# Decode trunk on Trainium2: wider moving operands in the sampled compression, chunk numbers made two stages earlier, gate products spread differently

## What is computed

```python
def compress_blocks(rows, w1, b1, w2):          # CMP_STRIDE 16, CMP_RATIO 2
    chunks = rows.reshape(b, n_chunks, CMP_STRIDE, g, d)
    part = jnp.einsum('bcjgd,ujde->ubcge', chunks, w1)
    hid = b1 + part[0, :, :n_cmp]
    for u in range(1, CMP_RATIO):
        hid = hid + part[u, :, u:u + n_cmp]
    return jnp.einsum('bcge,ef->bcgf', jax.nn.silu(hid), w2)

def full_rows(cache, new):
    past = cache[page_table].reshape(b, past_len, N_KV, HEAD_DIM)
...
    kc = compress_blocks(full_rows(ck_c, k_c), w1[0], b1[0], w2[0])
    vc = compress_blocks(full_rows(cv_c, v_c), w1[1], b1[1], w2[1])
```

## Time and profile before

| what | value |
|---|---|
| median of 3 runs | 2046.36 us (2042.62 to 2046.47) |
| the profiled execution's own time | 2048.14 us |
| its span | 2046.1 us |
| PE busy | 1841.1 us (90%) |
| DVE, ACT, POOL busy | 680.1, 560.5, 368.8 us |
| `compress_sample` in the trace | about 1139 to 1342.6 us |
| `attend_sample` in the trace | about 1342.6 to 1533 us |

### The profile page before, as it was taken

The page is one execution under the profiler, slowest core; times in us unless marked ns, Lnnn a source line. Parts: engine busy times, 40 slices in busy tenths (PEclk is TensorE's granted clock), DMA queues, the critical chain, the costliest instruction groups (busy, mean ns, idle before and its releaser), DMA issues. The chain is left out here.

```text
span 2046.1 us, 42386 instructions
## 1 busy us (share of the span) xinstructions
PE 1841.1 (90%) x18840; PEld 1228.6 (60%) x18840; DVE 680.1 (33%) x1448; ACT 560.5 (27%) x1148; POOL 368.8 (18%) x438
## 2 busy tenths in 40 slices
PE   7999689999999979689888489888999999899997
PEld 5666465666666645556666478875666666444443
DVE  3101354344443235066666445244120010111122
ACT  4111433334331200166665011122220000122223
POOL 0211331122220000044545211013200010000000
PEclk9999699999999989799999799888999999999999
DMA  4110100000000061350000775436732110400110
GB/s 138 52 31 11 28 3 12 22 13 13 12 13 23 14 149 21 134 125 2 2 2 1 226 231 178 177 101 147 174 85 103 42 41 21 166 21 21 41 41 21
DMA packets 116074, 135.96 MB, mean 66 GB/s; under 512 B 48220, under 2 KB 97061, under 8 KB 111326
## 3 DMA queue, kind: packets, MB, share of 16 engines
q1 hardware_dynamic: 106576, 83.95, 14.9%
q0 software_dynamic: 9216, 49.29, 7.7%
q10 hardware_dynamic: 102, 0.03, 0.0%
HBM read 120.64 MB, written 16.62 MB: 67 GB/s over the span
## 5 line engine op out<-in xcount | busy, mean ns | idle before, releaser
L709 PE MATMUL ps<-xnT,rw_side_w 128*128 128x344 f32 x576 | 202.3, 474 | 0.0
L448 PE MATMUL ps<-xnT,w_z 128*128 128x344 f32 x624 | 183.7, 456 | 2.3 <-DVE xnT L541 1.3
L448 PEld LDWEIGHTS ps<-xnT,w_z 128*128 128x128 f32 x624 | 118.9, 192 | 63.9 <-issue 3.1
L1822 POOL TENSOR_SCALAR probs<-probs,row_sums,gates 128x63 f32<-128x63 f32 (+6 forms) x148 | 95.0, 657 | 291.6 <-DVE row_sums L1782 291.6
L709 PEld LDWEIGHTS ps<-xnT,rw_side_w 128*128 128x128 f32 x576 | 99.5, 190 | 44.6 <-issue 11.1
L2094 PE MATMUL ps<-xnT,zT 128*128 128x344 f32 x384 | 123.9, 473 | 0.0
L2578 PE MATMUL ps<-xnT,ring_k 128*128 128x344 f32 x384 | 116.7, 458 | 2.2 <-PEq L81 2.2
L2582 PE MATMUL ps<-zT,ring_k 128*128 128x344 f32 x384 | 115.0, 452 | 0.0
L2762 PE MATMUL ps<-w_pg,h_T 128*128 128x512 f32 x256 | 111.3, 593 | 1.0 <-ACT h_T L2791 1.0
L2706 PE MATMUL ps<-w_out,mT 128*128 128x512 f32 x256 | 111.6, 593 | 0.5 <-DVE h_sample L2846 0.5
L1166 POOL TENSOR_TENSOR rw_Lb<-rw_Lm,level_mask 128x512 f32<-128x512 f32 x40 | 50.6, 1273 | 271.2 <-DVE rw_Lm L1325 261.2
(11 more groups left out here) (512 smaller groups left out, 2932.5 us busy)
## 6 DMA issues: line engine op xcount, KB each, us to landing
w_z<-in_w_in_dram SPq DMA_DIRECT2D x13, 512.0 KB, 3.8
xnT_kept<-xnT SPq DMA_DIRECT2D x1, 4128.0 KB, 12.7
xnT<-xnT_kept SPq DMA_DIRECT2D x1, 4128.0 KB
x_tok<-in_x_prompt_dram SPq DMA_DIRECT2D x8, 512.0 KB, 7.9
rw_side_w<-in_w_in_dram SPq DMA_DIRECT2D x16, 256.0 KB, 3.3
zT<-in_w_in_dram SPq DMA_DIRECT2D x8, 512.0 KB, 8.7
ring_k<-in_w_in_dram SPq DMA_DIRECT2D x8, 512.0 KB, 4.1
w_out<-in_w_out_dram SPq DMA_DIRECT2D x1, 4096.0 KB
```

The lines of the kernel that those rows point to most:

```text
L448: last = nc.tensor.matmul(k.ps[:, u % 6, 0:CG], w[:, n % w_ring, c, :], k.xnT[:, c, g * CG:(g + 1) * CG], start=(c == 0), stop=(c == KC - 1))
L709: ins = nc.tensor.matmul(k.ps[:, SIDE_BANKS[g % 2], 0:CG], w.side[:, t % 2, c, :], k.xnT[:, c, g % 3 * CG:(g % 3 + 1) * CG], start=(c == 0 ...
L1822: nc.gpsimd.tensor_scalar(every, every, ls[:, at:at + 1], k.gates[:, i, gate:gate + 1], ALU.mult, ALU.mult).then_inc(scaled, 1)
```

## The change

1. `convolve` takes both head groups in one moving operand of 256 columns. A pass is now half of the 16 token positions for one half of the channels: 8 x 4 matmuls, 4 passes, so 128 matmuls per unit. `project` still stands after the second pass and `score` after the third.
2. The chunk numbers are made in `turn_rows`. The tables and the page table are loaded by SP in `project_tokens`; PE's turn and spread stand after the second and fifth group of transposes in `turn_rows`. `compress_sample` starts with the gathers.
3. SP holds back the 16 transfers `cmp_w1v` until DVE has turned the first 4 gathers (`tr` 4).
4. In `attend_sample` 8 products more stand in `FILL_SELECT`, 8 new ones (`FILL_INDEX`) after the spread of the chosen rows, and 2 + 2 fewer in each of the 4 parts. `FILL_END` stays 16.

```diff
@@ project_tokens, SP
             sp.dma_start(k.dist_near[:], x.tab["dist"][:, W_SEL:]).then_inc(in_dist, 16)
+            sp.dma_start(k.pages_i[:], x.page_table).then_inc(in_page, 16)
+            for n in PAGE_TABLES:
+                sp.dma_start(k.tab[n][:], x.tab[n]).then_inc(in_page, 16)
             one.spread(sp)
@@ turn_rows, PE
                 last.then_inc(turned, 1)
+                if u == 1:
+                    pe.wait_ge(paged, 1)
+                    nc.tensor.transpose(k.ps[0:NPAGE, 5, 0:NB], k.pages[:], k.ident[0:NB, 0:NB]).then_inc(pt_ps, 1)
+                if u == 4:
+                    pe.wait_ge(paged, 2)
+                    for hf in range(2):
+                        last = nc.tensor.matmul(k.ps[:, 6, hf * NB:(hf + 1) * NB], k.tab["page_of"][:, hf, :], pages_t[:],
+                                                start=True, stop=True)
+                    last.then_inc(ix_ps, 1)
@@ turn_rows, DVE
+            nc.vector.tensor_copy(k.pages[:], k.pages_i[:]).then_inc(paged, 1)
             for u in range(1, 8, 2):
                 dve.wait_ge(turned, u + 1)
                 nc.vector.tensor_copy(k.kT[:, u // 2, 512:1024], k.ps[:, u % 4, :]).then_inc(out_v, 1)
+                if u == 1:
+                    dve.wait_ge(pt_ps, 1)
+                    nc.vector.tensor_copy(pages_t[:], k.ps[0:NPAGE, 5, 0:NB]).then_inc(paged, 1)
+            dve.wait_ge(ix_ps, 1)
+            for hf in range(2):
+                nc.vector.tensor_scalar(k.chunk_idx[:, hf, :], k.ps[:, 6, hf * NB:(hf + 1) * NB], 8.0, k.tab["mod8"][:, 0:1],
+                                        ALU.mult, ALU.add).then_inc(out_v, 1)
@@ compress_sample, SP
-            sp.dma_start(pt_i[:], x.page_table).then_inc(in_pt, 16)
             for n in CHUNK_TABLES:
                 sp.dma_start(k.tab[n][:], x.tab[n]).then_inc(in_tab, 16)
+            sp.wait_ge(tr, 4)
             assert load_block_weights(sp, x, w1[1], 1, in_w) == BLOCK_DMAS
@@ compress_sample, POOL
-            pool.wait_ge(idx_ok, 2)
@@ compress_sample, PE
-            def convolve(v, g, dh):
-                kv, s = units[v][0], v % 2
-                for j in range(16):
+            def convolve(v, part):
+                kv, s, dh = units[v][0], v % 2, part // 2
+                for j in range(8 * (part % 2), 8 * (part % 2) + 8):
                     for i in range(4):
                         h = slice(32 * i, 32 * i + 32)
-                        last = nc.tensor.matmul(k.ps[:, 4 * s + i, g * P:(g + 1) * P],
-                                                w1[kv][h, j, dh, :, :].rearrange("p u e -> p (u e)"),
-                                                ct[s][h, 4 * j + 2 * g + dh, :, :].rearrange("p m b -> p (m b)"),
+                        last = nc.tensor.matmul(k.ps[:, 4 * s + i, 0:256], w1[kv][h, j, dh, :, :].rearrange("p u e -> p (u e)"),
+                                                ct[s][h, 4 * j + dh:4 * j + dh + 3:2, :, :].rearrange("p g m b -> p g (m b)"),
                                                 start=(dh == 0 and j == 0), stop=(dh == 1 and j == 15))
...
-                convolve(v, 0, 0)
-                convolve(v, 0, 1)
+                convolve(v, 0)
+                convolve(v, 1)
                 if v:
                     project(v - 1)
-                convolve(v, 1, 0)
+                convolve(v, 2)
                 if v and units[v - 1][0] == 0:
                     score(v - 1)
-                convolve(v, 1, 1).then_inc(conv, 1)
+                convolve(v, 3).then_inc(conv, 1)
@@ attend_sample
-FILL_SOFT, FILL_SELECT, FILL_SPREAD = 8, 16, 8
-FILL_KEYS, FILL_SCORE, FILL_TURN = (4, 4, 4, 2), 8, 4
+FILL_SOFT, FILL_SELECT, FILL_INDEX, FILL_SPREAD = 8, 24, 8, 8
+FILL_KEYS, FILL_SCORE, FILL_TURN = (4, 4, 3, 1), 8, 3
...
+            mg.products(pe, FILL_INDEX)
             pe.wait_ge(w_lowd, 1)
...
-            mg.copies(act, FILL_SELECT)
+            mg.copies(act, FILL_SELECT + FILL_INDEX)
```

More of the change, by code:

```diff
@@ L252, in _ @@
             sp.wait_ge(in_dist, 32)
+            sp.wait_ge(in_page, 16 * (1 + len(PAGE_TABLES)))
         @block.tensor
@@ L337 @@
 RW_TABLES = ("ident2", "upper1", "lower", "level_mask", "gmask", "chunk_mask", "q_scale")
+PAGE_TABLES = ("page_of", "mod8")
 EARLY_TABLES = RW_TABLES + ("seen", "q_unscale")
@@ L1427, in turn_rows @@
         turned, out_a, out_v, gated = ctx.sem("rows_turned"), ctx.sem("rows_by_act"), ctx.sem("rows_by_dve"), ctx.sem("gates")
+        paged, pt_ps, ix_ps = ctx.sem("pages_float"), ctx.sem("pages_turned"), ctx.sem("pages_spread")
+        pages_t = ctx.enter_context(nc.sbuf_tensor("pages_t", [NPAGE, NB], F32))
         block = ctx.enter_context(nc.Block())
@@ L1870, in compress_sample @@
         kcT = sb("s_kcT", [P, 2, 256])
-        in_pt, in_tab, in_later, in_w, in_xn = (ctx.sem(n) for n in ("in_pages", "in_tab", "in_later_tabs", "in_cmp_w1v", "in_xnT"))
+        in_tab, in_later, in_w, in_xn = (ctx.sem(n) for n in ("in_tab", "in_later_tabs", "in_cmp_w1v", "in_xnT"))
         in_c = [ctx.sem(f"in_chunks{n}") for n in range(ring)]
-        prep, zeroed, pt_ps, ix_ps, idx_ok, qz, tr, conv, fd, hd, sd, w2p, w2o, scd, sco = (ctx.sem(n) for n in (
-            "sc_prep", "sc_zeroed", "pages_turned", "pages_spread", "idx_ready", "q_spread", "c_turned",
+        zeroed, qz, tr, conv, fd, hd, sd, w2p, w2o, scd, sco = (ctx.sem(n) for n in (
+            "sc_zeroed", "q_spread", "c_turned",
             "c_conv", "c_first", "c_hidden", "c_silu", "c_w2", "c_w2_out", "c_scored", "c_scores_out"))
@@ L2017, in _ @@
         def _(dve):
-            dve.wait_ge(in_pt, 16)
-            nc.vector.tensor_copy(pt_f[:], pt_i[:]).then_inc(prep, 1)
-            dve.wait_ge(pt_ps, 1)
-            nc.vector.tensor_copy(pt_t[:], k.ps[0:NPAGE, 4, 0:NB]).then_inc(prep, 1)
-            dve.wait_ge(in_tab, 16 * len(CHUNK_TABLES))
-            for hf in range(2):
-                dve.wait_ge(ix_ps, 2)
-                nc.vector.tensor_scalar(idx[:, hf, :], k.ps[:, 5, hf * NB:(hf + 1) * NB], 8.0, k.tab["mod8"][:, 0:1], ALU.mult,
-                                        ALU.add).then_inc(idx_ok, 1)
             dve.wait_ge(zeroed, 3)
@@ L2050, in scores @@
                 dve.wait_ge(scd, v + 1)
+                if v == 0:
+                    dve.wait_ge(in_tab, 16 * len(CHUNK_TABLES))
                 for bb in range(2):
@@ L2107, in copies @@
         self.out += count
-FILL_SOFT, FILL_SELECT, FILL_SPREAD = 8, 16, 8
-FILL_KEYS, FILL_SCORE, FILL_TURN = (4, 4, 4, 2), 8, 4
-FILL_END = 3 * KC * KC - 3 * FILL_SOFT - FILL_SELECT - 2 * FILL_SPREAD - 4 * (sum(FILL_KEYS) + FILL_SCORE + 2 * FILL_TURN)
+FILL_SOFT, FILL_SELECT, FILL_INDEX, FILL_SPREAD = 8, 24, 8, 8
+FILL_KEYS, FILL_SCORE, FILL_TURN = (4, 4, 3, 1), 8, 3
+FILL_END = 3 * KC * KC - 3 * FILL_SOFT - FILL_SELECT - FILL_INDEX - 2 * FILL_SPREAD - 4 * (sum(FILL_KEYS) + FILL_SCORE + 2 * FILL_TURN)
 def load_merge_weights(sp, k, x, f):
@@ L2947, in hybrid_trunk @@
         k.q_s = sb("q_s", [P, NPAIR, NB])
+        k.pages_i, k.chunk_idx = (early.enter_context(nc.sbuf_tensor(n, shape, I32)) for n, shape in (
+            ("pages_i", [NB, NPAGE]), ("chunk_idx", [P, 2, NB])))
+        k.pages, k.tab["mod8"] = sb("pages_f", [NB, NPAGE]), sb("mod8", [P, 2])
         cmp_w = ExitStack()
@@ L2956, in hybrid_trunk @@
             k.kvtok = psb("kvtok", [P, NT + 1, KVW])
+            k.tab["page_of"] = psb("page_of", list(x.tab["page_of"].shape))
             k.dist_sel, k.dist_near = zT[:, 12, 0:W_SEL], psb("dist_near", [P, W_WIN + W_CMP])
```

18 lines of the change are left out of this document (4 added, 14 removed).

## The result

| what | before | after |
|---|---|---|
| median, same chip | 2046.41 us (2042.62 to 2050.1, 4 runs) | 1994.55 us (1988.33 to 1999.77, 4 runs) |
| ratio | 1 | 0.9756, 95% interval 0.9715 to 0.9796 |
| profiled execution: its time, its span | 2048.14, 2046.1 us | 1996.48, 1994.5 us |
| instructions in all, on PE | 42386, 18840 | 38288, 16792 |

A forecast was written before the change was run, and what follows sets the result against it. PE, busy 90%, was taken to stall in `compress_sample` for its own instructions, fetched in blocks of 256 beside full DMA engines. Terms -5.0 - 35.7 - 9.7 + 1.2 = -49.2 us gave 1999 us; 8-in-10 range 1990 to 2016.

The forecast's parts named there:

- the units' term: The 8 units of `compress_sample` shrink from 170.9 to 135.2 us, -35.7 us, mostly gaps and the clock lost behind them.
- that leaves 0.6 us per block: Units: burst plus gap took 7.6 us against 7.0 of work per block; six blocks leave 3 us, plus 2 for clock.
- The width term: Units: 256 instructions of 54.8 ns take the same 14.0 us as 512 of 27.4; no difference, bounds +5 and -2 us.
- The entry: Entry of `compress_sample`: gathers start 4.5 us earlier, holding back `cmp_w1v` gives 0.5 (0 to 2); sum -5.0 us.
- `attend_sample` ahead of the loop: The fills close two idle places of PE before the loop; net -1.3 us, or +1.5 if the clock still falls.
- so DVE's chain slips by 0.65: Select fill in `attend_sample`: 8 products take 4.89 us where PE's idle place is 4.25, delaying DVE by 0.65 us.
- The loop: Four parts of `attend_sample`: 4 products leave each, 2.1 us per part, 8.4 us in all; another wait could lose 4.
- The parts that cost: `turn_rows` gains a transpose and two spreads, +1.2 us (0 to 2.5); three more DMAs in `project_tokens` cost nothing.
- A supply that stays short: Rival, 16%: blocks take longer than 7.6 us under denser loads, some 20 instead of 5 us of gaps remain; 2014 us.
- Gathers as the bound: Rival, 12%: `cmp_w1v` slows the gathers more, units 2 and 3 wait some 6 us more; 2005 us.
- Stops that belong to the unit: Rival, 6%: gaps are not the instruction supply and stay, only -13.5 us remain; 2035 us.
- Everything hidden: Rival, 3%: no gaps at all in the units and the lower width bound; 1991 us.

The follow-up runs named there:

- Experiment 6: Changed kernel with the old narrow convolve and only the first 8 of the 32 gathers, results wrong by that; 2003.43 us in a single run.
- experiment 9: Changed kernel with POOL's memsets behind the first gather, one gate product after each window turn, fewer after the loop's first two key steps; 1989.51 us, ratio 0.9742.
- experiment 2: Kernel before with the wide convolve alone; index making, `cmp_w1v` and fills as before; 2011.5 us, ratio 0.9818.
- Experiment 7: Changed kernel without SP's wait before `cmp_w1v`, so these loads run beside the first gathers; 1996.07 us in a single run.
- the repeat: Changed kernel unaltered, run once more beside the combined kernel on the same chip; 1992.24 us, ratio 0.9760.
- experiment 5: Changed kernel with a one-column partner matmul ahead of each wide one, one output off by a relative 0.44; 2224.3 us in a single run.
- experiment 4: Changed kernel with the old gate product counts and the old convolve; 2033.38 us, ratio 0.9947.
- the third experiment: Changed kernel with the old gate product counts, wide convolve kept; 2004.76 us, ratio 0.9779.

## Why the prediction was right, step by step

**The reading of the stops held.** The prediction's whole case was that `convolve` waited for its own instructions beside full DMA engines. Experiment 6 shows the part of the load by taking it away and nothing from PE, and the instruction queue shows the rest. Its row on the page (packets, MB, share of the engines), before:

```profile
q8 instruction: 149, 2.44, 0.5%
```

and after:

```profile
q8 instruction: 133, 2.18, 0.5%
```

Those are 16 packets fewer for 4096 fewer instructions of PE, so 256 instructions a packet. The trace keeps the start and length of each packet of this queue, and they can be laid beside the stops:

| run | PE goes on at | after a stop of, us | last packet starts | packet has landed | from landing to PE, us |
|---|---|---|---|---|---|
| before | 1177.44 | 2.28 | 1174.96 | 1176.13 | 1.31 |
| before | 1185.02 | 3.73 | 1182.55 | 1183.65 | 1.37 |
| before | 1226.05 | 1.46 | 1223.60 | 1224.48 | 1.57 |
| before | 1289.82 | 3.19 | 1287.44 | 1288.42 | 1.40 |
| experiment 6 | 1171.98 | 3.16 | 1169.08 | 1170.54 | 1.44 |
| experiment 6 | 1288.07 | 2.62 | 1285.64 | 1286.57 | 1.50 |
| experiment 9, loop | 1371.41 | 1.15 | 1368.60 | 1369.92 | 1.49 |

All 41 stops of this kind in the four traces with narrow matmuls and in the loop of the ninth experiment, down to stops of 0.2 us, end 1.24 to 1.67 us after such a packet has landed, while the packets start 3.3 to 8.2 us apart. The stops also stand on a grid: from 1177.44 on, the matmul records of before from one stop to the next number 128, 511, 127, 384, 511, 128, 383, 128, 383, 128 and 766, multiples of 128 (256 instructions with the weight loads) but for a missing record here and there. The packets also show where the time goes. In the block from 1177.44 to 1185.02 the packet starts 5.1 us after the block's first instruction, and takes 1.1 us; in the quiet units of experiment 6 a packet starts within some 1.2 us of a block's start, and takes 0.9 to 1.4 us. So it is the start that comes late beside other transfers, not the transfer that is slow.

The rule of the Trainium skill that I weighed against it ("Runtime: NRT & Kernel Launch", section "Instruction fetch mechanics") has the size right, blocks of 256. That the fetch is mostly hidden holds here for the wide matmuls, which have no stop, and not for the narrow ones, where it showed for 19.5 us in one stage.

**The size of the units' term was too small**, -35.7 against -42.3. The step that failed is "that leaves 0.6 us per block": 3 us of stops and 2 us of clock behind them were forecast to stay, and none did, under a DMA share of up to 1.10 (experiment 2 shows the same with `cmp_w1v` early). The 7.6 us of the earlier trace rows were a true fetch (5.1 to its start, 1.1 for the packet, 1.4 until PE went on), but the longest of the stage: the other blocks that ended in a stop and can be measured spanned 4.7 to 7.0 us, no more than the 7.0 us of work that a block now holds. Taking the longest for each of six blocks was the error, and with no stop there was no clock to lose behind one. None of the seven traces at this width without partners has a stop, so a fetch of over 7.0 us is rare. The cold start was the second part: unit 0 needed 15.5 us, 1.5 above the 14.0 of full clock, not 2.8 (up to 2.2 in the other traces). Together that is 6.3 of the 6.9 us between 135.2 and 128.3. The width term, no difference per column, held within the 0.6 that are left. The 3.6 us of experiment 6 do not add to it: they compare with narrow matmuls of 28.1 ns in whole units, where the sum had taken the 27.4 of its best row.

**The entry**, -5.0 against -6.1. The numbers' early making gave less than 4.5: 4.7 us became 0.8 and not 0.1, since POOL itself takes 0.68 us to its first gather, so 3.8. Holding back the weights gave more than the 0.5 I took: 19.4 us from gather to PE's start became 17.1, 2.3 us, just past my bound of 2. Experiment 7 confirms it with 2.4.

**`attend_sample` ahead of the loop**, -1.3 against +0.2. The step that failed is "so DVE's chain slips by 0.65". It set the fill's length against the idle place of one trace, with the fill starting when it did there. In the first profile DVE waited 3.76 us for PE, 3.5 more than before; in the repeat 0.56, 0.3 more. What moved the start was the clock in the window turns ahead of it, where the prediction looked at the clock only after `c_low`. The products behind `c_low` came out as priced, 4.89 us in every trace of the new counts. The mean of the six such traces, -1.0, is near the -1.3, and a single trace is not. **The loop**, -8.4 against -7.9: 2.0 us a part instead of 2.1, and no other wait opened.

**The parts that cost.** `turn_rows` +0.5 for +1.2, as PE's transpose and spreads took 0.19 and 0.61 us and the rest lay beside ACT:

```profile
853.34 0.19 PE L1449 MATMUL ps<-ident,pages_f 8*32 8x8 f32 x1
...
855.65 0.61 PE L1453 MATMUL ps<-pages_t,page_of 32*128 32x8 f32 x4
...
858.37 0.35 DVE L1481 TENSOR_SCALAR chunk_idx<-ps,mod 128x8 int32<-128x8 f32 x2
```

The spreads had 0.99 in the earlier trace rows, where PE had been idle; here it came from transposes. In `project_tokens` nothing, as forecast.

**The rivals.** A supply that stays short (2014) had its condition, the denser load, and not its effect. Gathers as the bound (2005): PE has no wait for DVE in any unit. Stops that belong to the unit (2035): experiment 6 excludes it. Everything hidden (1991, 3%) came true in the units: no stop at all. Its chance was set too low, because I took 7.6 us as the length of every fetch.

**The total.** The terms add up to -49.2 us, and the traces give -51.5, or 55 without the 3.6 us that code ahead of the change took more. So the units' 6.6 us too little and the entry's 1.1 were in part made up for by that code and by `attend_sample`, which is luck. The named 1999 also does not follow from the sum as it stands: 49.2 less than the median of 2046.36 would be 1997.2.

## What to carry to other kernels

Idle time of PE that ends with no event shown, after runs of short matmuls and beside a DMA share of 0.5 and more, can be late instructions. Look whether the runs between stops hold a multiple of 256 instructions, whether a stop ends just after a packet of the instruction queue has landed, and whether a unit without transfers has none. Two things took the stops away here: no other transfers (experiment 6), which a kernel that needs its data cannot have, and half the instructions for the same columns, which brought 35 to 42 us. Holding back one competing load brought 2.4 us, and none of it from the stops. Filling an idle place uses up the reserve that hid a late start: here the same fill gave up to 2.8 us or lost up to 1.0, by when the clock fell ahead of it. Judge such an edit by more than one trace, and leave the fill shorter than the idle place.

## What the runs showed that was not expected

- PE was busy without a break and stayed at the lower clock: 0.50 over whole units of 46.1 us, when every second matmul had one column (experiment 5). It was at 1.00 with the same wide matmuls alone.
- The same program loses its clock at different points: window turns slow from the fifth or the seventh of eight groups on, worth 3.0 us, and in experiment 4 from the third. So one trace of such a stretch says nothing to better than that.
- Code ahead of the first edit moved by up to 11 us between profiled executions: the first key matmul of `project_tokens` stood at 738.4 us in the repeated run and 749.4 in the third experiment. That is more than any part of this change but the units. The span less that start repeats better, 1250.1 us in the first profile of the changed kernel and 1248.4 in the second. Of those 11 us, 9.5 are already there at the first product of `rwkv_prompt` with `rw_side_w` (286.9 and 296.4 us). What makes them is open.
- With four row groups at work, 256 columns cost 54.8 ns an instruction, and 128 columns 28.1 ns where nothing stops them (experiment 6: 16.7 - 2.3 of other work for 512). The operand's two separate runs of 128 columns cost nothing that shows.
